# Delta rule with half of the heads on the other partition half, and key-square sums in four column groups

## What is computed

```
def l2_normalize(x):
    xf = x.astype(jnp.float32)
    return xf * lax.rsqrt(jnp.sum(xf * xf, axis=-1, keepdims=True) + L2_EPS)
```

```
lower = jnp.where(strict, jnp.einsum('bnhid,bnhjd->bnhij', k_beta, kc) * decay, 0.0)
tmat = lower + jnp.eye(CHUNK, dtype=f32)
u = lax.linalg.triangular_solve(tmat, v_beta, ...)
w = lax.linalg.triangular_solve(tmat, k_beta * jnp.exp(gc)[..., None], ...)
attn = jnp.einsum('bnhid,bnhjd->bnhij', qc, kc) * decay

def step(state, inp):
    q_n, k_n, u_n, w_n, g_n, a_n = inp
    v_new = u_n - jnp.einsum('bhcd,bhde->bhce', w_n, state)
    out = (jnp.einsum('bhcd,bhde->bhce', q_n * jnp.exp(g_n)[..., None], state)
           + jnp.einsum('bhij,bhje->bhie', a_n, v_new))
    state = (state * jnp.exp(g_last)[..., None]
             + jnp.einsum('bhcd,bhce->bhde', k_n * jnp.exp(g_last - g_n)[..., None], v_new))
    return state, out
```

## Time and profile before

| | |
|---|---|
| median of 3 runs | 1973.94 us (1973.82 to 1976.06) |
| profiled execution | 1973.8 us, its span 1972.0 us |
| PE busy | 1821.8 us (92%) |
| DVE busy | 1433.9 us (73%) |
| ACT busy | 1069.5 us (54%) |
| POOL busy | 358.7 us (18%) |
| mean granted TensorE clock | 0.968 |
| project, products of pairs 5 to 11 and what is between | 381.71 to 545.70 us |
| delta rule | 548.41 to 868.31 us |

### The profile page before, as it was taken

One profiled execution on the slowest core, in us unless ns is written; L12 is line 12 of the kernel. 1 busy time (PEld: TensorE's weight loads), 2 busy tenths in 40 slices (PEclk: granted clock), 3 DMA queues, 4 the chain that ended last, 5 costly groups with the idle time before them and its releaser, 6 DMA issues. The chain is left out here.

```text
span 1972.0 us, 35312 instructions
## 1 busy us (share of the span) xinstructions
PE 1821.8 (92%) x14136; PEld 1036.1 (53%) x14136; DVE 1433.9 (73%) x1790; ACT 1069.5 (54%) x1310; POOL 358.7 (18%) x230
## 2 busy tenths in 40 slices
PE   4999989999969999989999999489999999999965
PEld 1656644444459999954444455344444444444432
DVE  5555656858766666626765778689999988888938
ACT  3466643465433333333333311288888888888934
POOL 0000000111001211200000000124444444444400
PEclk9999999999989999999999999589999999999988
DMA  8500045752463232033314121399999999999935
GB/s 324 104 22 23 1 164 190 252 197 104 172 150 93 51 98 51 3 108 99 107 54 139 33 94 67 133 393 391 409 406 413 409 398 401 391 390 387 370 144 202
DMA packets 161716, 391.32 MB, mean 198 GB/s; under 512 B 25371, under 2 KB 102804, under 8 KB 132910
## 3 DMA queue, kind: packets, MB, share of 16 engines
q1 hardware_dynamic: 146574, 357.87, 50.2%
q0 software_dynamic: 15008, 31.56, 4.2%
HBM read 361.68 MB, written 48.68 MB: 208 GB/s over the span
## 5 line engine op out<-in xcount | busy, mean ns | idle before, releaser
L2281 PE MATMUL ps<-w_gate_up_split,gathered_t 128*128 128x512 f16 x1728 | 388.4, 382 | 9.0 <-ACT gathered_t L2355 5.4
L2447 DVE SCALAR_TENSOR_TENSOR w_gate_up_split<-w_staged,w_gate_up_split 128x2048 f16<-128x2048 f32 x144 | 328.2, 2289 | 58.4 <-ACT w_gate_up_split L2346 57.0
L2346 ACT ACTIVATE w_gate_up_split<-w_staged 128x2048 f16<-128x2048 f32 x144 | 274.6, 1908 | 46.6 <-PE ps L2281 16.0
L2281 PEld LDWEIGHTS ps<-w_gate_up_split,gathered_t 128*128 128x128 f16 x1728 | 167.9, 98 | 209.1 <-ACT gathered_t L2355 10.6
L219 PE MATMUL ps<-u_transposed,w_gates_split 128*128 128x512 f16 x1152 | 254.8, 383 | 5.7 <-PEq L144 3.0
L825 PE MATMUL ps<-u_transposed,w_dense_split 128*128 128x512 f16 x1152 | 250.5, 379 | 1.7 <-DVE w_dense_split L190 0.9
L2308 PE MATMUL ps<-w_down_split,hidden_t 128*128 128x512 f16 x864 | 193.9, 381 | 7.2 <-ACT hidden_t L2392 4.5
L219 PEld LDWEIGHTS ps<-u_transposed,w_gates_split 128*128 128x128 f16 x1152 | 113.3, 99 | 146.8 <-issue 15.0
L825 PEld LDWEIGHTS ps<-u_transposed,w_dense_split 128*128 128x128 f16 x1152 | 111.9, 98 | 142.3 <-issue 7.1
L2447 DVE SCALAR_TENSOR_TENSOR w_down_split<-w_staged,w_down_split 128x2048 f16<-128x2048 f32 x72 | 164.2, 2287 | 17.1 <-ACT w_down_split L2346 16.9
L2346 ACT ACTIVATE w_down_split<-w_staged 128x2048 f16<-128x2048 f32 x72 | 137.3, 1908 | 44.4 <-DMA w_staged<-in_w_down 22.9
(11 more groups left out here) (359 smaller groups left out, 2923.2 us busy)
## 6 DMA issues: line engine op xcount, KB each, us to landing
w_staged<-in_w_gate SPq DMA_DIRECT2D x72, 1024.0 KB, 11.5
w_staged<-in_w_up SPq DMA_DIRECT2D x72, 1024.0 KB, 10.9
w_staged<-in_w_down SPq DMA_DIRECT2D x72, 1024.0 KB, 10.9
w_dense_ring<-in_w_in SPq DMA_DIRECT2D x17, 1024.0 KB, 7.6
w_ada_ring<-in_w_ada SPq DMA_DIRECT2D x8, 2048.0 KB
w_gates_ring<-in_w_in SPq DMA_DIRECT2D x24, 512.0 KB, 6.5
qkv_scratch<-delta_output POOLq DMA_DIRECT2D x20, 512.0 KB, 3.4
attention_output<-qkv_scratch SPq DMA_DIRECT2D x8, 1024.0 KB, 6.1
```

The lines of the kernel that those rows point to most:

```text
L2281: last = pe.matmul(ps[:, GU[s] + j, :], xt[:, s, xp, k, :], w16[:, j, wp, k, :], start=(k == 0 and t == 0), stop=(k == KC - 1 and t == 2))
L2346: nc.scalar.activation(split(kind, 0, int(q)), staged(m, kind, int(q)), ACT.Identity, scale=W_SCALE).then_inc(hi_ok[kind + q], 1)
L2447: nc.vector.scalar_tensor_tensor(split(kind, 1, int(q)), staged(m, kind, int(q)), W_SCALE, split(kind, 0, int(q)), ALU.mult, ALU.subtract) ...
```

## The change

In the delta rule, heads 4 to 7 hold what belongs to the state (v_new, the decayed keys, attention_t, u) for step s on the other partition half than heads 0 to 3. The lists of heads run 0, 4, 1, 5 and so on, so that neighbours are on different halves. The inverse `t_` is kept on the opposite half from its transpose `tt`; the level product `nsb` is written to the half of the inverse. The two products of a level then start from the same half and go to different halves, and they are issued head by head, the first into banks 0 and 1, the second into 2 and 3. VectorE, ScalarE and POOL write to the other half where this asks for it, which splits some of their instructions. In the projection, the four key sums use 32 columns of ones each, and go to four groups of 32 partitions of one bank; one copy takes them out, into two buffers in turn, and one store writes them.

Three steps are split by partition half; nothing changes place. The diff without repeated parts:

```diff
@@ project: allocation, SyncE, TensorE
-        ssq = m.sb("k_square_sums", [1, T], ctx=ctx)
+        ssq = m.sb("k_square_sums", [P, 2, 512], ctx=ctx)
...
-                        for b in range(2):
-                            sp.wait_ge(ssq_out[b], 64)
+                        for side in range(2):
+                            sp.wait_ge(ssq_out[side], 32)
...
-                    pe.wait_ge(ssq_ok, 2 * n) if n >= 1 else pe.wait_ge(ada_ok, 4)
-                    for b in range(2):
-                        for half in range(2):
-                            last = pe.matmul(ps[0:1, 4 + 2 * b + half, :], m.const("ones")[:, 0:1], sq[:, b, half * 512:half * 512 + 512],
-                                             start=True, stop=True)
+                    if n >= 1:
+                        pe.wait_ge(ssq_ok, n)
+                    for i in range(4):
+                        last = pe.matmul(ps[32 * i:32 * i + 32, 6, :], m.const("ones")[:, 0:32], sq[:, i // 2, i % 2 * 512:i % 2 * 512 + 512],
+                                         start=True, stop=True)
@@ project: ScalarE, POOL
-                for b in range(2):
-                    if 2 * n + b >= 1:
-                        act.wait_ge(ssq_out[1 - b], (n + b) * 16)
-                    nc.scalar.activation(ssq[:].rearrange("p (h t) -> p h t", h=2), ps[0:1, 4 + 2 * b:6 + 2 * b, :], ACT.Identity
-                                         ).then_inc(ssq_ok, 1)
+                if n >= 2:
+                    act.wait_ge(ssq_out[n % 2], n // 2 * 16)
+                nc.scalar.activation(ssq[:, n % 2, :], ps[:, 6, :], ACT.Identity).then_inc(ssq_ok, 1)
...
+                    pool.dma_start(m.ssq_dram[2 * n:2 * n + 2, :].rearrange("b (h t) -> (b h) t", h=2), ssq[0:P:32, n % 2, :]
+                                   ).then_inc(ssq_out[n % 2], 16)
@@ delta_rule
+        crossed = [(rows[0], rows[1]), (rows[1], rows[0])]
+        at_rows = lambda g, s: rows[s ^ g]
+        out_rows = lambda g, s: rows[1 - (s ^ g)]
+        turned_pairs = [h for j in range(4) for h in (j, j + 4)]
...
-                for h in range(H):
-                    for r in rows:
-                        last = pe.matmul(ps[r, 4 + h // 4, wide4(h)], ttb[r, h, :], vt[r, h, :], start=True, stop=True)
+                for h in turned_pairs:
+                    for s, r in enumerate(rows):
+                        last = pe.matmul(ps[at_rows(h // 4, s), 4 + h // 4, wide4(h)], ttb[r, h, :], vt[r, h, :], start=True, stop=True)
...
-                        for r in rows:
-                            last = pe.matmul(ps[r, g, at4(h)], cm[r, k % 2, h, :], tt[r, h, :], start=True, stop=True)
+                        for r, q in crossed:
+                            last = pe.matmul(ps[q, g, at4(h)], cm[r, k % 2, h, :], tt[r, h, :], start=True, stop=True)
...
-                        for r in rows:
-                            last = pe.matmul(ps[r, 2 + g, at4(h)], t_[r, h, :], nsb[r, h, :], start=True, stop=True)
-                    if k < LEVELS - 1:
-                        for h in range(4 * g, 4 * g + 4):
-                            for r in rows:
-                                last = pe.matmul(ps[r, 2 + g, at4(h, 1)], nsb[r, h, :], t_[r, h, :], start=True, stop=True)
+                        for r, q in crossed:
+                            last = pe.matmul(ps[r, g, at4(h)], t_[q, h, :], nsb[q, h, :], start=True, stop=True)
+                        if k < LEVELS - 1:
+                            for r, q in crossed:
+                                last = pe.matmul(ps[q, 2 + g, at4(h)], nsb[q, h, :], t_[q, h, :], start=True, stop=True)
...
-                    for h in range(H):
+                    for h in turned_pairs:
+                        r = at_rows(h // 4, s)
                         last = pe.matmul(ps[:, 6 - 2 * s + h // 4, wide4(h)], kd[r, h, :], vn[r, h, :], start=True, stop=True)
...
-                for h in range(H):
-                    last = pe.matmul(ps[rows[1 - s], 4 + 2 * s + h // 4, wide4(h)], at[r, c % 2, h, :], vn[r, h, :], start=False, stop=True,
+                for h in turned_pairs:
+                    r = at_rows(h // 4, s)
+                    last = pe.matmul(ps[out_rows(h // 4, s), 4 + 2 * s + h // 4, wide4(h)], at[r, c % 2, h, :], vn[r, h, :], start=False, stop=True,
...
-                    last = nc.scalar.activation(wq[:, s, :, rows[s]], ps8(6 + s), ACT.Identity)
+                    for g in range(2):
+                        last = nc.scalar.activation(wq[:, s, heads(g), at_rows(g, s)], ps8(6 + s)[:, heads(g), :], ACT.Identity)
...
+                for g in range(2):
+                    r = out_rows(g, s)
+                    last = nc.scalar.activation(orow[r, heads(g), :], ps[r, 4 + 2 * s + g, :].rearrange("p (h t) -> p h t", h=4), ACT.Identity)
...
-                nc.vector.tensor_tensor(t_[:], cm[:, 0], over("ident_chunk"), ALU.add).then_inc(S("t0_ok"), 1)
+                for r, q in crossed:
+                    last = nc.vector.tensor_tensor(t_[q], cm[r, 0], over("ident_chunk")[r], ALU.add)
...
+                for r, q in crossed:
+                    last = nc.vector.tensor_tensor(kd[q, heads(1), :], ps4(7)[r], col(c, EKD, heads(1))[r].to_broadcast([CHUNK, 4, P]), ALU.mult)
```

More of the change, by code:

```diff
@@ L742, in project @@
         ada_bank = lambda n: {5: 5, 7: 7}.get(n, 4)
-        row_piece = lambda n: ssq[:, (n - 6) * 512:(n - 5) * 512] if n >= 6 else ada_row[:, n % 2, :]
+        row_piece = lambda n: ssq[0:1, n - 6, :] if n >= 6 else ada_row[:, n % 2, :]
         w_ada = a["w_ada"][0].rearrange("(k p) n -> p k n", p=P)
@@ L1073, in _ @@
                 if p - 1 in KEYED:
-                    for b in range(2):
-                        n = (p - 1 - KEYED[0]) * 2 + b
-                        pool.wait_ge(ssq_ok, n + 1)
-                        pool.dma_start(m.ssq_dram[n:n + 1, :], ssq[:]).then_inc(ssq_out[b], 16)
+                    n = p - 1 - KEYED[0]
+                    pool.wait_ge(ssq_ok, n + 1)
+                    pool.dma_start(m.ssq_dram[2 * n:2 * n + 2, :].rearrange("b (h t) -> (b h) t", h=2), ssq[0:P:32, n % 2, :]
+                                   ).then_inc(ssq_out[n % 2], 16)
                 if p == 9:
-                    for b in range(2):
-                        pool.wait_ge(ssq_out[b], 64)
+                    for side in range(2):
+                        pool.wait_ge(ssq_out[side], 32)
                     pool.dma_start(ssq_rows[:], m.ssq_dram.rearrange("h (c p) -> (h c) p", p=P)).then_inc(ssq_in, 16)
@@ L1206, in turn @@
                 if c >= 1:
-                    pe.wait_ge(S("n_ok"), c * 10)
+                    pe.wait_ge(S("tt_ok"), c * 10)
                 for g in range(2):
                     for h in range(4 * g, 4 * g + 4):
-                        for r in rows:
-                            last = pe.matmul(ps[r, g, at4(h)], t_[r, h, :], m.const("ident_chunk")[r, :], start=True, stop=True)
+                        for r, q in crossed:
+                            last = pe.matmul(ps[r, g, at4(h)], t_[q, h, :], m.const("ident_chunk")[q, :], start=True, stop=True)
                     last.then_inc(S("tt_mm"), 1)
@@ L1274, in write_state @@
             def write_state(c, s):
-                r = rows[s]
                 pe.wait_ge(S("vn_ok"), c * 2 + s + 1)
@@ L1368, in output @@
                 for s in range(2):
-                    last = nc.scalar.activation(m.o[:, :, c * P + s * CHUNK:c * P + (s + 1) * CHUNK], turned[:, :, rows[1 - s]], ACT.Identity)
-                last.then_inc(S("o_ok"), 1)
+                    nc.scalar.activation(m.o[:, heads(0), c * P + s * CHUNK:c * P + (s + 1) * CHUNK], turned[:, heads(0), rows[1 - s]], ACT.Identity)
+                nc.scalar.activation(m.o[:, heads(1), c * P:(c + 1) * P], turned[:, heads(1), :], ACT.Identity).then_inc(S("o_ok"), 1)
             def last_rows(b):
@@ L1426, in lower @@
                 step.settle()
[L1427 removed]
+                for r, q in crossed:
+                    last = nc.vector.tensor_tensor(t_[q], cm[r, 0], over("ident_chunk")[r], ALU.add)
+                last.then_inc(S("t0_ok"), 1)
                 part(c, 1)
@@ L1432, in lower @@
                     dve.wait_ge(S("o_mm"), 2 * (c - 1))
-                nc.vector.tensor_tensor(at[:, c % 2], ps8(3), dt_[:], ALU.mult).then_inc(S("at_ok"), 1)
+                nc.vector.tensor_tensor(at[:, c % 2, heads(0)], ps8(3)[:, heads(0)], dt_[:, heads(0)], ALU.mult)
+                for r, q in crossed:
+                    last = nc.vector.tensor_tensor(at[q, c % 2, heads(1)], ps8(3)[r, heads(1)], dt_[r, heads(1)], ALU.mult)
+                last.then_inc(S("at_ok"), 1)
             def level(c, k):
@@ L1441, in level @@
                     dve.wait_ge(S("x_mm"), c * 10 + 2 * (k - 1) + g + 1)
-                    nc.vector.tensor_tensor(tt[:, heads(g), :], part4(2 + g, 0), tt[:, heads(g), :], ALU.add).then_inc(S("tt_ok"), 1)
```

(13 more changed lines are left out.)

9 lines of the change are left out of this document (2 added, 7 removed).

## The result

1930.78 us (1928.67 to 1931.37, four runs) against 1974.6 us: ratio 0.9774, interval 0.976 to 0.9789. That lies inside the forecast range of 1911 to 1936 us, but 11 us above the forecast of 1920 us: of 54 us expected, 44 came. The number alone would fit rival B (1930 to 1936 us) better than the forecast's own case A (1914 to 1927 us), so the traces have to decide between them. The profiled execution took 1931.37 us, its span 1929.5 us against 1972.0. In the kernel after, some of TensorE's lines have a number one higher (L1224 was L1223, L1235 was L1234, L1285 was L1284); L1238 to L1281 keep theirs.

The account below looks back on a forecast made before the run. TensorE was taken to bound the projection and the delta rule's chunks. From 1973.8 us, -43.7 (delta rule) and -10.2 (projection) gave 1919.9, so 1920 us, range 1911 to 1936 us.

Parts of the forecast that it names:

- rival B: Levels: 22 ns is TensorE's issue floor, so a four-tile round costs 0.088 to 0.1 us; 1930 to 1936 us; chance 0.14.
- case A: Whole kernel as forecast, four tiles per 0.058 us in the levels; own range 1914 to 1927 us; chance 0.62.
- projection: Key sums as four column groups take two rounds instead of 8 issues: -2.55 us each, four times, -10.2.
- chunk 0: Delta rule's first chunk: levels wait for VectorE, shorter products give nothing, split inverse and attention_t cost +1.0 us.
- chunks 1 to 7: Delta rule: each chunk goes from 36.2 to 30.1 us, -6.1; seven chunks -42.7 us.
- behind chunk 7: Behind the last chunk: state update and attention product runs halve, -2.6 us; key rows 0.6 later; -2.0 net.
- C: Levels: VectorE binds, shorter levels leaving it less room; +0.5 to 1.1 us a chunk, 1924 to 1928 us; chance 0.12.
- VectorE's chain: Behind level 5: split k_decayed and inverse instructions cost +0.6 us each; after 1.39 slack, 0.7 a chunk is exposed.
- D: Levels: switching tile inside a run costs a drain like a change of shape; slower, 1991 us; chance 0.03.
- E: Projection: column groups do not overlap, or only in pairs, or VectorE's loop holds it; 1924 to 1930 us; chance 0.05.
- a clock of 1.00: Projection and six delta-rule chunks: granted clock read as 1.00, the 2.4 GHz level, in the profile before.
- The three runs that halve: Behind chunk 7: one state update run (L1281) and two attention product runs (L1284) halve on a full TensorE, -2.6 us.

Follow-up runs that it names:

- e3: The changed kernel with the solutions for u issued for heads 0 to 7 in plain order: 1925.78 us, ratio 0.975.
- e1: The kernel before with the projection's part of the change alone: 1964.39 us, ratio 0.9948.
- e10: The changed kernel with the 32 issues of the solutions for u done twice, same result: 1928.3 us, ratio 0.977.
- e2: The changed kernel with a level's two products one after the other for each half of the heads, not alternating by head: 1936.75 us, ratio 0.9808.
- e4: The changed kernel run again unedited, for a second profile: 1930.56 us, ratio 0.9777.
- e5: The changed kernel with the third piece of the gates' low split moved from chunk 6 to chunk 7: 1927.78 us, ratio 0.9757.
- e9: The changed kernel with the state update issued for heads 0 to 7 in plain order: 1936.74 us, ratio 0.9805.
- e6: The changed kernel with decayed keys made from ScalarE's copy instead of PSUM, and later, behind the next chunk's attention_t: 1916.56 us, ratio 0.97.
- e7: The changed kernel with the next stage's 48 products behind the last chunk spread over TensorE's waits there: 1922.9 us, ratio 0.974.
- e8: The changed kernel with the edits of e5, e6 and e7 together: 1914.95 us, ratio 0.9693.
- e11: e8 with ScalarE copying half of step 1's output rows ahead of level 4's product and the turned output ahead of level 5's: 1910.9 us, ratio 0.9666.
- e12: e11 with the second piece of the gates' low split moved to chunk 7 too: 1909.72 us, ratio 0.967.

## Why the prediction was right, and where it missed

| | forecast | measured |
|---|---|---|
| projection | -10.2 | -10.1; alone -9.7 |
| chunk 0 | +1.0 | +1.1 |
| chunks 1 to 7 | -42.7 | -38.9 |
| behind chunk 7, to the next stage's second piece | -2.0 | +1.7 |
| elsewhere | 0 | +3.8 |
| sum | -53.9 | -42.4 |

The measured column is taken from the two profiles, whose spans are 1971.97 and 1929.54 us.

The mechanism was right: the traces show case A's. The number was not in A's own range, and it lies in the whole range only because that was opened up to 1936 us for rivals B and C. Of these, C had a small part (chunk 6), B none. The 11 us that are missing have four causes, which follow: the clock, chunk 6, the tail, and scatter in stretches that nobody edited.

**Right: the chunk.** Four levels gave 4 x 0.92 = 3.7 (forecast 3.75), u 0.86 (0.87), the two stretches from the state update to the second step of the level behind it 2 x 1.44 = 2.9 (1.79 + 1.75 - 0.9 = 2.6). Given back at VectorE's chain were 0.65 before w and 0.44 before the turn, less 0.22 at the read of the state, 0.9 (0.7 forecast), and 0.5 at the output rows and the key rows (0.5). The sum is 6.0 us, where 6.1 were forecast. A round over four tiles takes as long as one over two, 0.058 us. This excludes B, which needs 0.088 to 0.1. It excludes D too: the tile changes at every issue and no time goes with it. E is excluded by the key sums, four column groups in two rounds of 0.43 us. Writes to the other partition half cost what their columns cost (L1431, 1.39 us for two of 64x512).

**Right: chunk 0.** VectorE is what this chunk waits for. From the first inverse to the end of level 4 it is busy for 21.5 of 21.7 us before and for 23.1 of 23.4 us after. The split inverse and attention_t cost 1.3 us of the added 1.7 (1.0 was forecast); 0.8 us came back because the chunk's first steps waited less for a transfer. The clock (0.81 before, 0.63 after) cannot explain the difference: e3 has 0.80 and takes 39.32 us. e1's chunk 0 is short (37.45 us) because its first inverse starts after 6.8 us instead of 8.0, behind a shorter wait for the same transfer. What can move it by as much is where POOL's work falls. The changed kernel's chunk 0:

```profile
560.46 2.87 POOL L1537 TENSOR_TENSOR state_decayed<-state,exp_g_last 128x1024 f32<-128x1024 f32 x1
561.61 2.27 DVE L1421 TENSOR_TENSOR level_parts<-minus_lower,table 128x512 f32<-128x512 f32 x1
```

and e10's, with the same VectorE list and 37.45 us:

```profile
561.61 1.10 DVE L1421 TENSOR_TENSOR level_parts<-minus_lower,table 128x512 f32<-128x512 f32 x1
562.12 2.34 POOL L1537 TENSOR_TENSOR state_decayed<-state,exp_g_last 128x1024 f32<-128x1024 f32 x1
```

**Missed: "a clock of 1.00".** The sum took the clock of before as given. Chunk 4 lost 1.55 us to a clock of 0.95, and the tail 3.4. The evidence differs between the two.

- In the tail it is strong. Seven profiles have a wait of 1.7 to 2.6 us ahead of w there (the changed kernel, e2, e3, e4, e5, e9, e10). In all seven the clock is at half for 3.4 or 6.8 us, beginning 4.0 to 5.6 us behind the start of u. The seven with a wait of 0.94 us or less (before, e1, e6, e7, e8, e11, e12) have no fall in the first 26 us behind the start of u. e6 removed the wait, e7 filled it with products, and either way the fall was gone.
- In the chunks there is no more than a tendency. TensorE had been idle for 0.75 us a chunk and is for 1.9. All five profiles of kernels that leave it idle for 1.9 us in every chunk (the changed one, e4, e5, e7, e9) have one chunk of 2 to 5 at 0.95, at 1.6 us each, and the other nine have none there. But chunk 3 of e10, idle for 1.9 us, and chunk 6 of the changed kernel, idle for 3.7, have the full clock, and chunk 7 of e2, idle for 1.5, has 0.95. That idle time brings these falls is not shown.

**Missed: the tail, +1.7 instead of -2.0.** The waits came nearly as forecast. From u to w it now takes 798.38 - 794.73 = 3.65 us, where it took 844.22 - 841.31 = 2.91: +0.7, with +0.6 forecast. The three runs that halve gave 2.4 (2.6 forecast). What the sum left out is that the longer wait brings a fall of the clock: w and the twelve L219 behind it take 3.3 us more. That is nearly all of the 3.7 us.

**Missed: chunk 6, 2.1 us, a case of C.** I took VectorE's slack from chunk 4 alone. Chunk 6 has three pieces of the gates' split in VectorE's list (28.03 instead of 23.97 us busy already before), and at 30 us a chunk that decides. e5 and e12 show it: with the third piece moved half of the surplus goes, with the second moved too the rest.

**Elsewhere, 3.8 us:** 0.9 lay in front of the first edit, 0.4 between the projection and the delta rule, 2.5 behind the delta rule, where nothing was edited. From the end of the tail to the end of the span it took 1100.6 us before, 1103.1 after and 1102.3 in e4, the same program; over all profiles it goes from 1098.5 (e10) to 1105.3 (e11). This is scatter, and its cause stays open.

## What to carry to other kernels

Runs of matmuls that name different quarters of the array, and write to different banks, overlapped by themselves here, by about three issues per quarter (e2, e3, e9). So first give neighbouring runs different quarters, then alternate within a run. When a step off TensorE gets shorter, look for who waits behind it: here u's gain was given back in full until VectorE's list was reordered. Recompute slack in the chunk with the most side work, not in a typical one. And where the saved work leaves TensorE waiting, look at the granted clock behind the wait: here a wait of 2.6 us was followed by 6.8 us at half clock.

## What the hardware showed unexpectedly

- Starts of TensorE's issues in four tiles are on average 15 ns apart (64 in 0.94 us), some of them 7 ns. So the 22 ns of the earlier trace rows were no floor. The Trainium skill (TensorE: Matmul & The Clock Gate, on 56 against 53.3 ns) has about 25 ns; here it does not hold.
- A run was overtaken by the next one where that names other tiles, and other banks, by up to three issues a tile (e2, e3, e9).
- VectorE's L1421 took 2.27 us beside POOL's L1537 and 0.69 us alone.
- Runs of one program differ by up to 9.5 us (e10, where the slower ones have the lower mean clock; in e3 the order is not so).
